# GpSimd's 128x1024 elementwise instructions issued as four 128x256 pieces in a hybrid decoder block

## The reference, cut to what matters

```python
mod = silu(c) @ w_ada + b_ada          # 6 vectors of 1024: shift, scale, gate, twice (adaLN)
h = rms_norm(x, norm1_g) * (1 + scale1) + shift1
proj = h @ w_in                        # q_lat, k, v, indexer keys, recurrence inputs, two gates
out_a = sparse attention: 8 heads of 64, each query keeps its top 128 causal keys
out_b = rms_norm(hgrn2(silu(b_q), b_f, b_i)) * silu(b_g)     # 4 heads of 128, gated recurrence
merged = sigmoid(gate_a) * (out_a @ w_proj_a) + sigmoid(gate_b) * (out_b @ w_proj_b)
x = x + gate1 * (merged @ w_out)
h2 = rms_norm(x, norm2_g) * (1 + scale2) + shift2
x = x + gate2 * (square(relu(h2 @ w_mlp1 + b_mlp1)) @ w_mlp2 + b_mlp2)
```

## Time and profile before

| | |
|---|---|
| median of 3 runs | 1005.82 us (1004.93 to 1009.44) |
| span of the profiled execution | 1008.2 us |
| PE, DVE, ACT, POOL busy | 895.3, 467.6, 370.0, 380.1 us |
| POOL: weight differences (L372) | 126 instructions, 304.4 us, mean 2417 ns |
| POOL: adaLN additions (L389) | 28 instructions, 67.0 us, mean 2392 ns |

### The profile page before, as it was taken

The page is one execution under the profiler, slowest core; times in us unless marked ns, Lnnn a source line. Parts: engine busy times, 40 slices in busy tenths (PEclk is TensorE's granted clock), DMA queues, the critical chain, the costliest instruction groups (busy, mean ns, idle before and its releaser), DMA issues.

```text
span 1008.2 us, 11253 instructions
## 1 busy us (share of the span) xinstructions
PE 895.3 (89%) x3855; PEld 700.9 (70%) x3855; DVE 467.6 (46%) x692; ACT 370.0 (37%) x527; POOL 380.1 (38%) x189
## 2 busy tenths in 40 slices
PE   3699899898778666699999999699999999999998
PEld 2477578686666555566656777478888888888886
DVE  4814789791897989533332851522211112221000
ACT  2534443444134342456553122444421214343111
POOL 3324233334245463511112433134444444444440
PEclk9699999999878796879999999799999999999999
DMA  9823223324244351321111222223333323233302
GB/s 361 225 52 84 63 65 103 84 68 141 63 126 140 92 174 56 103 63 43 42 42 42 83 84 84 63 63 104 99 96 96 104 84 103 87 100 105 98 27 84
DMA packets 144550, 95.69 MB, mean 95 GB/s; under 512 B 8198, under 2 KB 138628, under 8 KB 143492
## 3 DMA queue, kind: packets, MB, share of 16 engines
q1 hardware_dynamic: 143104, 95.18, 32.0%
q10 hardware_dynamic: 1412, 0.07, 0.1%
HBM read 93.13 MB, written 2.10 MB: 94 GB/s over the span
## 4 chain that ended last, share of the span: by engine, by line
PE 74%; DVE 19%; DMA 2%; ACT 2%; issue 1%; POOL 0%; SPq 0%; DVEq 0%; ACTq 0%; POOLq 0%
PE bank L1042 19%; PE bank L1044 18%; PE bank L1043 18%; PE bank L1183 2%; DMA ada_raw<-in_w_ada 2%; PE bank L1184 2%; DVE hg_qk L905 2%; PE bank L1185 2%; DVE hg_qk L906 2%; PE bank L1264 2%; DVE hg_e L908 2%; PE bank L1290 2%; DVE bT L909 2%; PE bank L1208 1%; DVE hg_at L889 1%
## 5 line engine op out<-in xcount | busy, mean ns | idle before, releaser
L372 POOL TENSOR_TENSOR w_lo<-w_raw,w_hi 128x1024 fp32r<-128x1024 f32 x126 | 304.4, 2417 | 507.7 <-ACT w_hi L435 507.6
L1042 PE MATMUL bank<-h_hi,w_hi 128*128 128x512 f32 x544 | 220.1, 405 | 17.2 <-DVE h_lo L763 15.9
L1043 PE MATMUL bank<-h_lo,w_hi 128*128 128x512 f32 x544 | 214.0, 393 | 0.0
L1044 PE MATMUL bank<-h_hi,w_lo 128*128 128x512 f32 x544 | 213.6, 393 | 0.0
L435 ACT ACTIVATE w_hi<-w_raw 128x1024 fp32r<-128x1024 f32 x126 | 132.4, 1052 | 162.1 <-PE bank L1044 160.5
L1042 PEld LDWEIGHTS bank<-h_hi,w_hi 128*128 128x128 f32 x544 | 103.2, 190 | 49.9 <-issue 20.0
L1043 PEld LDWEIGHTS bank<-h_lo,w_hi 128*128 128x128 f32 x544 | 103.6, 190 | 22.2 <-issue 1.9
L1044 PEld LDWEIGHTS bank<-h_hi,w_lo 128*128 128x128 f32 x544 | 103.4, 190 | 22.0
L389 POOL TENSOR_TENSOR ada_acc<-ada_acc,ada_raw 128x1024 f32<-128x1024 f32 x28 | 67.0, 2392 | 91.9 <-ACT ada_raw L594 90.1
L1042 PE MATMUL bank<-u_hi,w_hi 128*128 128x512 f32 x256 | 99.9, 390 | 0.0
L1044 PE MATMUL bank<-u_hi,w_lo 128*128 128x512 f32 x256 | 99.6, 389 | 0.0
(11 more groups left out here) (210 smaller groups left out, 1174.8 us busy)
## 6 DMA issues: line engine op xcount, KB each, us to landing
w_raw<-in_w_mlp SPq DMA_DIRECT2D x128, 256.0 KB, 3.0
w_raw<-in_w_in SPq DMA_DIRECT2D x88, 256.0 KB, 3.3
ada_raw<-in_w_ada SPq DMA_DIRECT2D x32, 512.0 KB, 4.0
ada_raw<-in_w_ada SPq DMA_DIRECT2D x8, 1024.0 KB, 9.1
w_raw<-in_w_out SPq DMA_DIRECT2D x16, 256.0 KB, 3.0
x_nat<-in_x SPq DMA_DIRECT2D x4, 512.0 KB, 6.1
w_raw<-in_w_proj_a SPq DMA_DIRECT2D x8, 256.0 KB, 2.9
w_raw<-in_w_proj_b SPq DMA_DIRECT2D x8, 256.0 KB, 3.2
```

Source lines behind the costliest of these rows:

```text
L372: nc.gpsimd.tensor_tensor(w_lo[:, s], w_raw[:, s], w_hi[:, s].bitcast(F32), ALU.subtract).then_inc(lo_ready, 1)
L1042: mm(bank[b][:], w_hi[:, slot, j], rhs_hi(i), start=f, stop=False)
L1043: mm(bank[b][:], w_hi[:, slot, j], rhs_lo(i), start=False, stop=False)
L1044: end = mm(bank[b][:], w_lo[:, slot, j], rhs_hi(i), start=False, stop=l)
```

## The change

Both POOL instructions are cut along the free axis. A weight difference over `w_lo[:, s]` (eight blocks of 128) becomes four over two blocks each. An adaLN addition over 1024 columns becomes four over 256 columns. The waits ahead of each stay as they are, once for all four; the semaphore rises with the last of the four. The same elements are computed with the same operation.

```diff
             def split_lo(n, s):
                 pool.wait_ge(hi_ready, n + 1)
-                nc.gpsimd.tensor_tensor(w_lo[:, s], w_raw[:, s], w_hi[:, s].bitcast(F32),
-                                        ALU.subtract).then_inc(lo_ready, 1)
+                for j in range(0, 8, 2):
+                    end = nc.gpsimd.tensor_tensor(w_lo[:, s, j:j + 2], w_raw[:, s, j:j + 2],
+                                                  w_hi[:, s, j:j + 2].bitcast(F32), ALU.subtract)
+                end.then_inc(lo_ready, 1)
...
                     pool.wait_ge(ada2_used, i)
-                    nc.gpsimd.tensor_tensor(ada_acc2[:], ada_acc2[:], ada_raw2[:, i % 3],
-                                            ALU.add).then_inc(ada2_used, 1)
+                    for c in range(0, D, D // 4):
+                        end = nc.gpsimd.tensor_tensor(ada_acc2[:, c:c + D // 4], ada_acc2[:, c:c + D // 4],
+                                                      ada_raw2[:, i % 3, c:c + D // 4], ALU.add)
+                    end.then_inc(ada2_used, 1)
```

## The result

The change took the median from 1005.72 us to 981.99 us (981.12 to 984.95, four runs beside four of the kernel before): ratio 0.976, interval 0.974 to 0.979. The forecast was 981, in a range of 970 to 1000.

A forecast was written before the change was run, and what follows sets the result against it. PE leads the chain, but in seven recurrence stretches DVE blocked by POOL sets the end. Savings 25.1 there plus 2.9 outside, minus losses 1.0 and 2.0, give 25.0: median 1005.8 to 981 us, range 970 to 1000.

The forecast's parts named there:

- What bounds: In seven stretches of the recurrence on the chain, DVE two-input operations wait for the running POOL instruction, about 2.1 us each.
- The contended pitch: Start-to-start time of DVE operations each let in between two POOL pieces: 0.84 us after the change instead of 2.49.
- f: Cost paid per POOL instruction whatever its size: taken as 0.10 us, possibly near 0.0, at most about 0.29.
- the second, fourth and sixth stretch: Recurrence spans 275.00 to 291.67, 326.08 to 338.27, and one ending at 384.07: 3.1, 4.6 and 5.3 us saved.
- the first, third, fifth and seventh stretch: Recurrence spans beginning at 249.24, 303.86, 349.15, and a last one like that from 303.86: 2.6, 3.4, 2.7, 3.4 us saved.
- the backlog behind the reciprocal: Second difference of heads 0 and 2 ends later and meets DVE operations that were free before: 2.0 us lost.
- The fourth stretch: Recurrence, from L905 at 326.08 to reciprocal L857: falls from 12.2 to about 7.6 us, 4.6 saved.
- Lost at the end: Recurrence end: last two additions each 0.3 us longer, and L861 getting in pushes POOL by about 0.4; 1.0 lost.
- Elsewhere: Gains outside the recurrence: 1.2 us at the start, 0.9 at L786, 0.8 in the merge; together 2.9.
- No way in between pieces: Rival: DVE waits for all four pieces at some 27 blocked operations, 8 us slower, 1014; chance 0.12.
- The gain swallowed in half: Rival: PE and ACT become the bound half the time, or pieces are dear; 12 to 14 us remain, about 993; chance 0.15.
- No change through dear pieces: Rival: pieces cost so much that no gain is left, needing 1.14 us per piece; about 1006, chance 0.04.

## Why the prediction was right

**What bounds.** Right. With only the additions cut the recurrence loses its long stalls and 23 us; with only the differences cut it loses nothing. The stalls were where the windows of the earlier trace rows had them.

**The pitch and the way in.** The contended pitch was put at 0.84 and is 0.87; the four pieces of an addition, all contended, at 3.36, and by POOL's timeline the four from 295.93 take 3.36, and 3.50 to the start of the next addition. Alone four pieces last 2.83 instead of 2.60, which puts f at 0.14 (the pieces start 0.70 apart), between the ends of 0 and 0.29. Letting DVE in costs POOL 0.17, and the two errors cancel in part. POOL's busy time was to rise by about a tenth and rose by 26% in these two groups: a piece's recorded span holds its wait for DVE, which I had not counted. It cost nothing, as POOL's time was covered. For the same reason the pieces' mean is 0.79 and not near 0.65, and 44 of the 616 last over 1 us, which I had named as a sign of being wrong: that sign was badly chosen, for a span that holds a wait is not the price of a piece. (In the sum, an f of 0.085 gives 51 x 0.011 = 0.6 us, not below half.)

**The stretches.** From L885 to the reciprocal of heads 1 to 3 the table shows 12.1 us saved, and 1.5 more on the way from L920 there; the second, fourth and sixth stretch were to give 3.1, 4.6 and 5.3, together 13.0. From the reciprocal to L920 and in head 0, 8.1 were saved; the first, third, fifth and seventh stretch were to give 12.1, less the 2.0 for the backlog behind the reciprocal, 10.1. So 2.0 more are missing than the backlog term had. In head 1 the way from the reciprocal to the third stretch took 14.5 us (281.75 to 296.21) instead of 12.2 (291.67 to 303.86). Of these 2.3, 1.0 is the backlog: L861 (now L865) lasts 1.12 instead of 0.69, and the L905 behind it (now L909) 0.94 instead of 0.42. It is the same in heads 2 and 3, 2.9 together, where I had 2.0 in two heads. The other 1.3 is a wait for PE that had no term. DVE waits 1.55 us for PE's L1212 (the former L1208), where it had waited 0.26; in head 2 it waits 1.55 as well, where its own stall had covered that, and in head 3 as long as before. The fourth stretch, named as a sign, fell from 12.2 to 7.8 (7.6 expected). The whole stage was put at 22.1 net and gave 21.6, in part by luck: from the end of the last L920 to the last reciprocal 1.5 was saved (it waits 1.74 for PE there instead of 3.80), for which the forecast had no term. The third stretch itself took 6.4 and not 6.9.

**Lost at the end.** Put at 1.0; the last reciprocal to the modulation vectors grew by 1.7, confirmed by the run with these additions whole. The step that missed was the last addition: both the operations of L861 and L865 (L865 and L869 after) get into it, not one.

**Elsewhere.** Put at 2.9, and the run without pieces there lost about 3, within a rough interval. But its parts were not right. At the start I had 1.2: the first unit's last product comes 14.9 us after the modulation sum with pieces and 14.6 without, so nothing was gained; the stalls of L741 and L753 were traded for eight contended operations of 1.1 to 1.2 us instead of 0.75. In the key norms the L786 of 2.17 became one of 1.10 (L790), near the 0.9 I had put. What was gained in the indexer scores and the merge is not shown. It can't be told from the drift: the kernel with only the additions cut, whose instructions up to the recurrence are those of before, came to PE's first score products of the indexer (`kiT`, `qiT`) at 128.69 us in its profiled execution, and the kernel before at 132.38, 3.7 us later.

**The rivals.** No way in between pieces: it did not happen in the change, by the timelines and by the run with waits. But it exists: with 128 columns it kept out the operation over 8 columns, for 6.70 and 2.72 us. So the sign that I named, a DVE instruction of 2.4 or more, came in the kernels with eight pieces at these places. The gain swallowed in half: not here; PE's wait for `hg_qk` fell from 42.7 to 25.4 us. DVE's waits for PE took a part behind the reciprocals (above), and with two pieces most of it. No change through dear pieces: a piece costs 0.70, not 1.14.

The Trainium skill's dispatch rule in "GPSIMD Engine Reference" (section "Instruction dispatch"), by which cores run on into the next POOL instruction, does not keep DVE out between pieces of 256 columns. Whether it is behind the 6.70 us with 128 columns no run here shows, since no row shows cores apart. The Trainium skill's lock for a whole instruction in "SBUF — State Buffer" (the sections on ports) agrees with the operations of the levels in all these kernels, with a stall that follows the length of the POOL instruction: 2.1, 1.07, 0.53 and 0.26 us for 1024, 512, 256 and 128 columns (durations 2.57, 1.48, 0.95, 0.68, less 0.42). The operation over 8 columns, kept out over 16 and 6 such instructions in a row, waited for more than one.

## What to carry to other kernels

An engine with 0% of the chain can still set its length by holding a port: look for one shape of instruction with a wide spread of durations, and lay the two timelines side by side. Cutting the long instruction pays only so far as pieces are left over for a time when the other engine doesn't want the port; walk through the operations to see how many pieces they meet, since a cut in two gave 0.2%, one in four 2.4% and one in eight no more. A small piece can also keep a small operation out altogether, so look at the timelines of every stage after a finer cut. Leave whole what lies on the chain itself or what nobody contends with.

## What the runs showed of the hardware

- A POOL two-input operation costs about 0.14 us for every further instruction it is cut into: 2.39, 2.83 and 3.39 us for one, four and eight pieces of the same 1024 columns.
- A DVE operation over 8 columns got in between POOL pieces of 256 and 512 columns in rows without a pause (0.18 to 0.71 us), and in all three cases in which it met rows of 128 columns it waited until the row was over: 6.70, 2.72 and 2.72 us.
- Letting a 128x256 DVE operation in costs POOL 0.17 us with pieces of 256 columns (0.87 against 0.70 from start to start) and 0.19 with pieces of 128 (0.60 against 0.41).
- A DVE CAST of 128x512 from SBUF to SBUF meets the pieces too: in the merge it lasted 0.43 us before, when the whole difference was over, and 0.75 in all eight units after, with a piece running:

```profile
L991 DVE CAST h_hi<-sig_a x8: 751/755/757, 524.8 to 562.8; - x8
```

- A POOL addition over 8 columns lasted 0.20 us when nothing contended, against 0.10 for a memset of one column.
